# Up and down weights by column halves, smaller last loads, and a final norm by column halves on two queues

## The reference, cut to what matters

```python
g = xb @ w_gate[e] + b_gate[e]          # per expert, 1024 x 1024, float32
u = xb @ w_up[e] + b_up[e]
g = jnp.minimum(g, 7.0); u = jnp.clip(u, -7.0, 7.0)
out = ((u + 1.0) * g * jax.nn.sigmoid(1.702 * g)) @ w_down[e] + b_down[e]
...
x = x + y                               # y: each token's gated sum of outs
return rms_norm(x, norm_final_g)
```

## Time and profile before

| | |
|---|---|
| median of 3 runs | 1104.78 us (1104.24 to 1105.2) |
| the profiled execution | 1104.63 us, its span 1102.8 us |
| PE busy | 1047.2 us, 5412 matmul records |
| DVE, ACT, POOL busy | 293.6, 129.8, 9.6 us |
| moved by DMA | 438.16 MB, mean 397 GB/s over the span |

### The profile page before, as it was taken

The page is one execution under the profiler, slowest core; times in us unless marked ns, Lnnn a source line. Parts: engine busy times, 40 slices in busy tenths (PEclk is TensorE's granted clock), DMA queues, the critical chain, the costliest instruction groups (busy, mean ns, idle before and its releaser), DMA issues.

```text
span 1102.8 us, 12757 instructions
## 1 busy us (share of the span) xinstructions
PE 1047.2 (95%) x5412; PEld 503.2 (46%) x5412; DVE 293.6 (27%) x608; ACT 129.8 (12%) x241; POOL 9.6 (1%) x17
## 2 busy tenths in 40 slices
PE   9999999999999999999999988989898979998896
PEld 8999996634433443344342422433243324332332
DVE  5677888420302121121111111211103020202022
ACT  2212350310000001001000100001000100000012
POOL 2000000000000000000000000000000000000000
PEclk9999999999999999999999999999999999999999
DMA  9974377899999999999999999999999999999996
GB/s 340 399 317 153 131 292 304 336 427 428 437 427 431 432 434 428 433 435 429 433 433 431 429 433 435 429 433 434 431 429 433 434 428 435 434 428 431 426 426 255
DMA packets 26654, 438.16 MB, mean 397 GB/s; under 512 B 4992, under 2 KB 6272, under 8 KB 9472
## 3 DMA queue, kind: packets, MB, share of 16 engines
q1 hardware_dynamic: 26048, 435.05, 93.1%
q10 hardware_dynamic: 576, 2.69, 0.6%
HBM read 436.28 MB, written 1.05 MB: 397 GB/s over the span
## 4 chain that ended last, share of the span: by engine, by line
PE 62%; DMA 35%; DVE 1%; issue 1%; ACT 0%; another core or an unknown queue 0%; DVEq 0%; SPq 0%
DMA ring<-in_experts 35%; PE ps L2021 24%; PE ps L2070 12%; PE ps L1592 6%; PE ps L1931 3%; PE ps L2079 3%; PE ps L1766 2%; PE ps L1831 2%; PE ps L1587 2%; PE ps L1637 1%; PE ps L1572 1%; PE ps L2059 1%; PE ps L1940 1%; ACT region_va L842 0%
## 5 line engine op out<-in xcount | busy, mean ns | idle before, releaser
L2021 PE MATMUL ps<-ring,xT 128*64 128x512 f32 x2044 | 458.4, 604 | 26.2 <-DMA ring<-in_experts 26.2
L2021 PEld LDWEIGHTS ps<-ring,xT 128*64 128x64 f32 x2044 | 144.2, 139 | 312.9 <-issue 281.5
L2070 PE MATMUL ps<-ring,region_va 128*64 128x512 f32 x1024 | 229.8, 599 | 20.0 <-ACT region_va L842 10.7
L2070 PEld LDWEIGHTS ps<-ring,region_va 128*64 128x64 f32 x1024 | 73.3, 137 | 154.7 <-issue 128.0
L1481 DVE TENSOR_SCALAR g<-ps 128x1024 f32<-128x1024 f32 x16 | 19.6, 1224 | 348.4 <-PE ps L2021 342.6
L1592 PE MATMUL ps<-ring 128*128 128x128 f32 x672 | 77.0, 276 | 0.1
L1592 PEld LDWEIGHTS ps<-ring 128*128 128x128 f32 x672 | 75.8, 192 | 0.9 <-DVE ring L961 0.3
L1427 DVE TENSOR_TENSOR xT<-ps,g_ffn 128x512 f32<-128x512 f32 x30 | 20.7, 691 | 191.0 <-PE ps L1931 191.0
L1503 DVE TENSOR_SCALAR region_va<-ps 128x512 f32<-128x512 f32 x32 | 22.1, 691 | 181.2 <-PE ps L2021 181.2
L1931 PEld LDWEIGHTS ps<-sel,x 128*128 128x128 f32 x480 | 55.4, 192 | 9.5 <-issue 9.5
L2079 PE MATMUL ps<-g,g_T 128*128 128x512 f32 x128 | 59.2, 605 | 0.0
(11 more groups left out here) (267 smaller groups left out, 546.5 us busy)
## 6 DMA issues: line engine op xcount, KB each, us to landing
ring<-in_experts SPq DMA_DIRECT2D x77, 4096.0 KB, 46.3
ring<-in_experts SPq DMA_DIRECT2D x28, 2048.0 KB, 12.4
ring<-in_head SPq DMA_DIRECT2D x13, 2048.0 KB, 12.8
ring<-in_experts SPq DMA_DIRECT2D x13, 1024.0 KB, 8.6
ring<-in_first SPq DMA_DIRECT2D x7, 384.0 KB, 6.6
ring<-in_experts SPq DMA_DIRECT2D x5, 512.0 KB, 8.8
ring<-in_experts ACTq DMA_DIRECT2D x2, 1024.0 KB, 9.8
ring<-in_experts SPq DMA_DIRECT2D x1, 1536.0 KB, 6.8
```

The lines of the kernel that those rows point to most:

```text
L2021: last = mm(bank(banks + half)[rows, :], xT[:, 2 * m + c, rows], weights[:, k], start=False, stop=m == 3 and c == 1, skip_group_check=True)
L2070: last = mm(bank(first + half)[rows, :], hTm[:, 2 * m + c, rows], w[:, c, half, k], start=m == 0 and c == 0, stop=m == 3 and c == 1, skip_ ...
```

## The change

- Up and down weights are laid out in HBM by column halves: loads 4 and 5 are the left 512 columns of up (all 8 chunks), 6 and 7 the right ones, 8 and 9 the left ones of down, 10 and 11 the right ones. Gate is as before.
- The first half of the hidden result is transposed between loads 6 and 7, the second in the middle of load 8. ACT copies the left down result after load 9.
- In odd pairs (1, 3, ... 15) the right half of down is laid out in two groups of 256 columns: load 10 is the third quarter of the columns, load 11 the fourth. Odd pairs but the last run both groups as one matmul over 2 x 256 columns; the last runs them one after the other, in steps of 256 columns, with scatters in between.
- Pair 14's units 4 and 5 come in loads of 2 MB. In pair 15 loads 7 to 10 come in two pieces of 1 MB, load 11 in four of 512 KB.
- Pairs 13 and 14 stand behind the loop on PE, written out.
- The final norm goes by column halves: left halves of both tiles are added and squared early (DVE), DVE adds the right ones by quarters; ACT squares tile 0's right half, DVE tile 1's; POOL and ACT scale both left halves, ACT issues their stores; DVE scales both right halves, SP issues those.

The diff, cut to its core:

```diff
+W256 = W512 // 2
+CLOSING_HALVED = (7, 8, 9, 10)
+SPLIT_UNITS = (4, 5)
...
             def load_last(row):
                 p = LOADS_PER_PAIR - 1
-                load_columns(row, p, 0, SLOT_COLS // 2, last_rows)
-                load_columns(row, p, 2 * D, 3 * D, last_left)
-                load_columns(row, p, 3 * D, 4 * D, unit_loaded[UNITS - 1])
+                for k in range(4):
+                    load_columns(row, p, k * D, (k + 1) * D, last_quarters[k] if k < 3 else unit_loaded[UNITS - 1])
+            def load_by_halves(row, p):
+                load_columns(row, p, 0, SLOT_COLS // 2, closing_rows[p])
+                load_columns(row, p, SLOT_COLS // 2, SLOT_COLS,
+                             unit_loaded[p // 2] if p % 2 else slot_loaded[SLOT_OF[p]])
...
-                        if not (closing and q or i is None or (opening and n == PAIRS_PER_ITER and m == 0)):
+                        if not (closing and (q or m in SPLIT_UNITS) or i is None or (opening and n == PAIRS_PER_ITER and m == 0)):
...
             for a in range(NT):
-                for half in range(2):
-                    cols = slice(half * W512, (half + 1) * W512)
-                    sp_.wait_ge((fin_done0, fin_done)[a], half + 1)
-                    sp_.dma_start(out_d[a * P:(a + 1) * P, cols], x3[:, a, cols]).then_inc(stored, 16)
+                sp_.wait_ge(fin_done, a + 1)
+                sp_.dma_start(out_d[a * P:(a + 1) * P, W512:D], x3[:, a, W512:D]).then_inc(stored, 16)
...
+                    used = it * LOADS_PER_ITER + LOADS_PER_PAIR * (q + 1)
+                    act.wait_ge(load_used, used + LOADS_PER_PAIR - 2)
+                    nc.scalar.copy(o_s[:, 0:W512], bank(first)).then_inc(o_ready, 1)
+                    if closing and q == PAIRS_PER_ITER - 1:
+                        act.wait_ge(load_used, used + LOADS_PER_PAIR - 1)
+                        nc.scalar.copy(o_s[:, W512:W512 + W256], bank(first + 1)[:, 0:W256]).then_inc(o_third, 1)
+                        act.wait_ge(load_used, used + LOADS_PER_PAIR)
+                        nc.scalar.copy(o_s[:, W512 + W256:D], bank(second)[:, 0:W256]).then_inc(o_ready, 1)
...
+            act.wait_ge(y_added, 2 * NT + 1)
+            nc.scalar.activation(fin_junk[:, 0:W512], x3[:, 0, W512:D], ACT.Square,
+                                 accum_out=fin_ssq[:, 2:3]).then_inc(ssq1_ready, 1)
             for a in range(NT):
+                act.wait_ge(fin_sums_ready, a + 1)
+                nc.scalar.activation(std[:, a:a + 1], fin_ssq[:, 2 + a:3 + a], ACT.Sqrt, scale=1.0 / D,
                                      bias=fin_bias[:, a:a + 1]).then_inc(fin_std, 1)
+            for a in range(NT):
+                act.wait_ge(rstd_ready, a + 1)
+                act.wait_ge(fin_g, a + 1)
+                nc.scalar.activation(x3[:, a, 0:W512], xg[:, a * W512:(a + 1) * W512], ACT.Copy,
+                                     scale=rstd[:, a:a + 1]).then_inc(fin_left, 1)
+                act.wait_ge(fin_left, a + 1)
+                act.dma_start(out_d[a * P:(a + 1) * P, 0:W512], x3[:, a, 0:W512]).then_inc(stored_left, 16)
...
+            for a in range(NT):
+                add_experts(a, a, 0, W512)
+            for a in range(NT):
+                dve.wait_ge(y_added, a + 1)
+                final.settle()
+                final.step(final_squares(a, 0))
...
+            for a in range(NT):
+                add_experts(2 + a, a, W512, W512 + W256)
+            for a in range(NT):
+                add_experts(4 + a, a, W512 + W256, D)
+            dve.wait_ge(y_added, 3 * NT)
+            final_squares(1, 1).then_inc(fin_sums_ready, 1)
...
+                def right_columns():
+                    loaded(LOADS_PER_PAIR - 2)
+                    w = unit(UNITS - 1).rearrange("p (g c k n) -> p g c k n", g=2, c=KC, k=2)
+                    for c in range(KC):
+                        last = down([w[:, :, c, k, :] for k in range(2)],
+                                    lambda rows: bank(first + 1)[rows, :].rearrange("p (g n) -> p g n", g=2), c)
+                    last.then_inc(load_used, 2)
+                def closing_quarter(g, bank_of):
+                    m = LOADS_PER_PAIR - 2 + g
+                    w = loaded(m).rearrange("p (c k n) -> p c k n", c=KC, k=2)
+                    for c in range(KC):
+                        if g == 0 and c == KC // 2:
+                            pe.wait_ge(o_ready, n * 2 + 1)
+                            scatter(0, 0, W512).then_inc(sc_done, 1)
+                            whole_loaded(m)
+                        if g == 1 and c in (2, 4):
+                            pe.wait_ge(last_quarters[c // 2], 32)
+                        if g == 1 and c == 6:
+                            pe.wait_ge(o_third, 1)
+                            scatter(0, W512, W512 + W256).then_inc(sc_done, 1)
+                            pe.wait_ge(unit_loaded[UNITS - 1], unit_count(n, UNITS - 1))
+                        last = down([w[:, c, k, :] for k in range(2)], lambda rows: bank(bank_of)[rows, 0:W256], c)
+                    last.then_inc(load_used, 1)
+                half_of_columns(0)
+                if last_pair:
+                    closing_quarter(0, first + 1)
+                    scatter(1, 0, W512).then_inc(sc_done, 1)
+                    closing_quarter(1, second)
+                    scatter(1, W512, W512 + W256).then_inc(sc_done, 1)
+                    pe.wait_ge(o_ready, n * 2 + 2)
+                    for a in range(NT):
+                        pe.wait_ge(y_added, NT + a + 1)
+                        scatter(a, W512 + W256, D).then_inc(sc_done, 1)
```

More of the change, by code:

```diff
@@ L624, in _ @@
             pool.wait_ge(ld_gfin, 16)
[L625 to L628, removed]
+            for a in range(NT):
+                pool.wait_ge(y_added, a + 1)
+                nc.gpsimd.tensor_tensor(xg[:, a * W512:(a + 1) * W512], x3[:, a, 0:W512], gfin[:, 0:W512],
+                                        ALU.mult).then_inc(fin_g, 1)
         @block.scalar
@@ L2019, in gate_or_up @@
                                 rows = slice(k * SLOTS, (k + 1) * SLOTS)
-                                weights = aside_w if first_pair and 4 * which + m == ASIDE_LOAD and c == half == 1 else w[:, c, half]
-                                last = mm(bank(banks + half)[rows, :], xT[:, 2 * m + c, rows],
-                                          weights[:, k], start=False,
+                                weights = aside_w if first_pair and m == ASIDE_LOAD and c == half == 1 else w[:, c, half]
+                                last = mm(bank(banks + half)[rows, :], xT[:, 2 * m + c, rows], weights[:, k], start=False,
@@ L2023, in gate_or_up @@
                                           stop=m == 3 and c == 1, skip_group_check=True)
[L2024 to L2027 removed]
+                            if first_pair and ((c, half) == (0, 1) or m == 0 and (c, half) == (0, 0)):
@@ L2061, in transpose_hidden, with down @@
                     last.then_inc(ht_done, 1)
-                transpose_hidden(0)
+                gate(first)
+                if first_pair:
+                    start_y()
+                up(second)
+                pe.wait_ge(gt_ready, n + 1)
                 if q == 1 and not last_pair:
+                    gather_next()
                     pe.wait_ge(xT_ready, n * 2 + 4)
-                def down(w, m, half, c):
+                def down(weights, out, c):
                     for k in range(2):
@@ L2110, in expert_pair, with scatter @@
-                for a in range(NT):
-                    for half in range(2):
-                        scatter(a, half)
+                        last = mm(out(rows), hTm[:, c, rows], weights[k], start=c == 0, stop=c == KC - 1,
+                                  skip_group_check=True)
+                    return last
+                def scatter(a, lo, hi):
+                    half = lo // W512
+                    at = half * W512
+                    return mm(bank(Y_B + 2 * a + half)[:, lo - at:hi - at], g_T[:, a * P:(a + 1) * P], o_s[:, lo:hi],
+                              start=False, stop=True, skip_group_check=True)
@@ new lines, in half_of_columns @@
+                def half_of_columns(half):
+                    for m in range(2):
+                        w = loaded(8 + 2 * half + m).rearrange("p (c k n) -> p c k n", c=4, k=2)
+                        if half == 0:
+                            pe.wait_ge(hT_ready, n * 2 + m + 1)
+                        for c in range(4):
+                            if last_pair and c == 2:
+                                whole_loaded(8 + 2 * half + m)
+                            last = down([w[:, c, k, :] for k in range(2)], lambda rows: bank(first + half)[rows, :],
+                                        4 * m + c)
+                            if half == m == 0 and c == 1:
+                                transpose_hidden(1)
+                        last.then_inc(load_used, 1)
```

233 lines of the change are left out of this document (101 added, 132 removed).

## The result

The changed kernel takes 1107.48 us (median of 13, 1106.81 to 1108.37) against 1104.78 us (median of 13 before). The ratio is 1.0024, with a 95% interval of 1.0017 to 1.0031: slower by 2.7 us. The forecast was 1104.0, with a range from 1101.8 to 1106.2; the measured median lies 1.3 us above the range. The profiled execution took 1107.28 us, with a span of 1105.4.

What follows compares the result with a forecast made beforehand. The weight stream was taken to bound the kernel, with PE late next: last two steps at 1092.3 plus a 9.9 us tail end at 1102.2 against 1102.8, a 0.6 us gain, so 1104.0 us, range 1101.8 to 1106.2.

Steps and rivals of the forecast that it cites:

- S: Start of pair 15's last two down steps on PE, forecast at 1092.3 us, 1.6 us after the last weight landing.
- the signs that it named: Prediction wrong if the last step waits for DMA, 256-column steps take over 0.45 us, or the stream's rate changes.
- Loads, bytes and sizes: Weight stream: same bytes in smaller pieces cost +0.4 us, moving the last landing to 1090.7 us.
- SP's queue: SP's load issues: held longer by a full queue, last issue some 17 us before its landing, no gap, 0.
- The body of the loop: Moved transposes and column groups in the pairs: small shifts on PE, hidden by the weight stream, 0.
- Pair 14 and 15 on PE: Pair 15 starts 3.5 us earlier; PE catches up and idles for load 10 from about 1082.6 to 1083.2 us.
- From there to the last landing: PE's steps, scatters and switches from 1083.3 us sum to 9.0 us, so PE is late by 1.6 us.
- The tail: From the start of the last two steps through final norm and stores to the span's end: 9.9 us, before 12.4.
- Narrow steps: Slower rival: 256-column steps show their weight loads, 0.28 us a step over 16 steps, +4.5 us, 1108.5; chance 0.06.
- small pieces: Slower rival: each 0.5 MB weight piece takes 2.7 us instead of 1.24, four cost +5.8 us, 1109.8; chance 0.02.
- the queue didn't run dry: Denies a slower rival: SP issues quarters too late, 3 us for each late one, 1107; chance 0.04.
- the granted clock: Clock-drop rival: some 3.5 us at the lower level in the last pair, +1.7 us, 1105.7; counted within the forecast's 0.65.

Runs made afterwards that it cites:

- e7: The change with pair 14's units whole, pairs 13 and 14 back in PE's loop, and without the further rounds of experts; 1104.23 us, ratio 0.9995.
- e5: The change without the further rounds (every engine's count load, branch and the code behind it left out); 1105.72 us, ratio 1.0011.
- e1: The kernel before with pairs 13 and 14 written out behind PE's loop, nothing else changed; 1105.85 us, ratio 1.0008.
- e2: The change with pair 14's units 4 and 5 as whole 4 MB loads, pairs 13 and 14 still written out; 1107.47 us, ratio 1.0021.
- e3: The change with pair 14's units whole and pairs 13 and 14 back in PE's loop; 1106.07 us, ratio 1.0012.
- e11: e7 with pair 15's two left scatters cut from 512 to 64 columns, a probe with an incomplete result; 1103.02 us, ratio 0.9987.
- e14: e3 with PE reading the round count ahead of pair 15 and branching behind it as before; 1105.82 us, ratio 1.0011.
- e9: e3 with PE reading the round count and branching ahead of pair 15, which stands twice; 1111.69 us, ratio 1.0066.
- e12: The kernel before with PE's branch ahead of pair 15 and tile 0's stores issued by ACT; 1112.36 us, ratio 1.0067.
- e10: The kernel before with PE reading the round count and branching ahead of pair 15; 1112.24 us, ratio 1.0071.
- e4: The change with all four stores issued by SP; 1107.18 us, ratio 1.0022.
- e6: The kernel before without the further rounds of experts (count load, branch and code behind it left out); 1103.92 us, ratio 0.9994.

## Why the prediction was wrong

It summed to an end at 1102.2 us; the span was 1105.4. Of the 3.2 us, 1.7 lie before S and 1.5 behind it. The order of waits was forecast rightly and none of the signs that it named came up: the last step didn't wait for DMA, a step of 256 columns took 0.43, and between the jolts the loads kept their 4.89 us. Two terms were wrong, and behind both stands one thing that the sum left out, the loading of instructions.

*Loads, bytes and sizes: "Sum +0.4 us: the last landing moves to 1090.7".* This step failed. The sizes were priced well: from pair 14's unit 5 to the last quarter e7 takes 59.2 us against 58.9 before (0.2 forecast), and e5, whose large jolt fell elsewhere, needs 19.7 us for the four 2 MB loads against 19.5 for two units (0.17 forecast). What was missing was a term: new code. The prediction has no word on pairs 13 and 14 being written out, and so put it at nothing. The landing was 1092.2, 1.5 us behind the forecast, and the two jolts are 1.5 us. e1 shows the writing out alone, with one jolt; e2 and e3 show it taken back, 1.4 us.

*SP's queue.* Right: SP was held, for 4.2 us at most issues of 1 MB and 2.1 us at the last ones of 512 KB, and the last weight piece went out at 1070.4, 21.7 us ahead of its landing. No gap.

*The body of the loop: 0.* Right for the matmuls and waits; in e3 and e7, where the loop holds pairs 13 and 14, the units land 9.71 us apart up to pair 14, as before.

*Pair 14 and 15 on PE.* Right. PE waits 0.56 us for load 10 in the changed kernel. In e3, without the split units, PE has no such wait and is as late behind the last landing (1.7 us) as with them (1.8), so splitting pair 14's units gained nothing here.

*From there to the last landing: 9.0 us.* Measured 9.2 (1084.72 to 1093.96), 1.8 us behind the landing where 1.6 was forecast. e11 shows that it is PE's: with shorter scatters it is 0.6. The terms of this stretch add up to 8.9, not 9.0; nothing hangs on it.

*The tail: S + 9.9.* Measured 11.4. The last issue came at S + 6.3 (6.8 forecast): ACT's first issue took 0.37, not the 1.23 that the forecast allowed for in part. The term that failed is "Landing 2.3 to 2.9, median 2.7": 4.6, beside an instruction load. That it is the load is shown over eight traces, in which the last issue is at S + 6.3 each time: with a load beside the stores (the change, e2, e3, e14) the span ends at S + 11.4 to 11.5, without (e5, e7, e9, e11) at S + 9.5 to 9.6.

With both costs taken away, in e7 (no further rounds, pair 14's units whole), the sum comes out: S at 1092.2 (1092.3 forecast) and a span of 1101.8 (1102.2). The median, 1104.23, is 0.2 us from the forecast time, but the profiled execution was 0.7 below that median, so the fit of the positions is in part luck. The distances, 1.7 us from landing to S and 9.5 from there, are not.

*The rivals.* Narrow steps showed no weight loads (0.43 a step), small pieces paid no fixed price (1.2 to 1.3 us from one 512 KB landing to the next), the queue didn't run dry, and the granted clock stayed at its higher level from 1015.5 us to behind PE's last matmul. The Trainium skill (DMA: Bandwidth & Descriptors, section Issuing engines are not separate DMA queues) says that issuing from several engines saves no more than the time of the issues. The runs agree: in e12 the last store is issued 0.3 us earlier behind the first scatter than in e10 (7.3 and 7.6 us), and the medians differ by 0.1 us.

Open stays why some instruction loads jolt the landings and others of the same kernel don't: of four loads two did in the change (0.8 and 1.05 us) and in e2 (0.4 and 1.1), one in e1 (1.0), one in e4 (1.0) and one in e5 (1.4, and 0.1 at another). If the one engine that serves a load isn't the last one at that time its delay is hidden; the rows don't say which engine served which, so this is argued, not shown. Where e6's 0.9 us come from is clearer: e10 keeps the branch, has no load beside its stores and takes the same 10.6 us from the first scatter to the end as e6, where the kernel before takes 11.4. As far as one profile of each can tell, it is the load beside the stores, not the branch.

## What to carry to other kernels

Where the DMA stream is the bound, code is part of the stream: a loop body written out costs instruction loads on the same engines (here 0.4 to 1.4 us for each that delayed a landing), and a branch near the end brings its load down beside the last stores. Before pricing an unrolled pair at nothing, count the instruction rows of the DMA view and where they fall. A pause of PE can also cost more than itself, through the clock behind it (e10: 5.7 and 2.3 us). And a tail that gets shorter can move into such a load; look at what stands beside the last transfer, not only at its own row.

## What the runs showed that I had not expected

Between 366 and 957 us, in the loop, the changed kernel has no 16 KB instruction load at all; behind it they come every 23 to 35 us. Such a load takes 0.9 to 1.1 us of one DMA engine there and up to 1.4 at the end of other kernels (1.41 before), where a whole 16 KB row of weights took 0.61. The last store's landing grew by 1.8 us beside a load of 0.96; why by twice its length is open. PE's branch over code took 3.4 us at the end of the changed kernel, unseen, since nothing followed on PE, and 6.1 us in e10, where something did.
